# Router matrix stationary, rows' products first in the first expert, third expert from one-hot rows

## The chip, the cores and the metric

One core of a Trainium2 chip (trn2). The metric is the device time of one execution in microseconds. TensorE multiplies, VectorE (DVE), ScalarE (ACT) and GpSimd (POOL) compute elementwise, SyncE (SP) issues most of the transfers; POOL also issues all indirect ones (gather, scatter, scatter with add).

## The reference

One layer over 1024 tokens of width 1024, all float32: a mixer (short convolution, stick-breaking attention, gated linear attention), an output projection, a layer norm, then a mixture of experts and a second layer norm. What matters here:

```python
x = layer_norm(ALPHA * x + mix, ln1_g, ln1_b)         # mix = concatenated mixers @ w_out
scores = sigmoid(x @ router_w)                        # (1024, 16)
sel = scores + router_bias                            # best group of 4 by its two best; top 2 in it
gate = top-2 scores / their sum                       # zero for the other 14 experts
for e in range(16):
    h = silu(x @ w1[e]) * (x @ w3[e])                 # (1024, 512)
    y = y + gate[:, e:e+1] * (h @ w2[e])
out = layer_norm(ALPHA * x + y, ln2_g, ln2_b)
```

Only the two chosen experts of a token have a gate that isn't zero, so the kernel computes each expert for its own tokens alone. An output in float32 needs products more exact than one pass gives: a big product is made of three (hi x hi, hi x lo, lo x hi, with hi a rounded copy and lo the rest, lines 675 to 677, `mm3`).

## The kernel before

**Projection, first norm, router** (lines 887 to 924 on PE). Over the eight tiles of 128 tokens, iteration i of PE does: the eight transposes of tile i-2 of x1 (the normed x); 48 matmuls of the output projection of tile i; the router's product of tile i-2: x1T (128x128 per k) is stationary and 16 columns of the router's matrix `rw` move, eight calls. In float32 a call becomes two machine matmuls. ACT copies x1T out of PSUM between them, in a loop of its own order (lines 1255 to 1272); behind the last projection it also converts the first four weight pieces of expert 0 (`piece_hi`, 1.0 us each) ahead of the last x1T copy. `lg_ps` counts the tiles whose logits are there; at eight ACT takes the exponential (line 1276) and DVE begins the routing.

**Routing** (DVE, lines 1558 to 1635): sigmoid, ranks, masks, gates. Then PE counts each token's place in its expert (line 930), giving every token of an expert a slot: 160 slots for an expert, 128 "rows" (A) and 32 "spare" ones (B). For the first two experts a one-hot compare (`oneh`) and small PE products (lines 940 to 945) give the token of each slot at once (`firstA`, `firstB`), so that POOL gathers their x1 rows without the table. For all others the table `slot_tokens` in DRAM is written by 16 small indirect DMAs (`scatter`, line 569: a token's number and gate to its slot), and is read back by `load_table` (5 small DMAs for an expert), turned to indices by `quarters`, used by `gather`; `gates` puts the gates into `slotG`, and `add_rows` adds the expert's result to `sum_scratch` by two indirect DMAs (yB, yA).

**The experts** (`pe_block`, lines 981 to 1022). Each has 12 weight pieces of 512 KB: w1 (0 to 3), w3 (4 to 7), w2 (8 to 11). SP loads piece p of the next expert into the same raw buffer `er` as soon as the piece was split (`el_ok`) and read raw (`raw_done`). ACT makes `eh`, DVE `el`. PE does, in order: the spare rows' products with the raw weights (`spare_gu`, 64 calls = 128 small matmuls in four column groups, 32 of them each; raises `raw_done`), the rows' products with w1 and w3 (`rows_gu`, 24 big matmuls each), transposes of hB, of the next expert's gathered rows (rounds 0 and 1 of `x_transposes`), of hA, and of the next spare rows (round 2), then the products with w2, spare rows first (32 small ones) and then 24 big ones. Expert 0 is written out ahead of a loop over 1 to 14; expert 15 behind it. In the first block round 2 of the transposes comes first (`ROUNDS_FIRST = (2, 0, 1)`), since the spare rows' products only need that one. ACT's and DVE's order (`act_block`, `dve_block`) follow: pieces 4 and 5, then the spare rows' silu (which waits for `raw_done` of eight pieces) and multiply, then pieces 6 and on.

**POOL's order** behind the routing: gather of expert 0, scatter of the first choices (8 DMAs), gather of expert 1, scatter of the second choices, wait until the table has landed; then tables of experts 0, 1, 2, indices, gather 2, gates 0, adds of expert 0, and from there `step`: load table b, gates b-2, indices b, gather b, adds b-2. yA, yB and `slotG` are single buffers: ACT and DVE write the next expert's result once `y_out` says that the last one's adds have landed.

## Time and profile before

| what | value |
|---|---|
| runs shown | 1025.86 us median of 3 (1021.03 to 1026.15) |
| profiled execution | 1031.45 us, span 1029.6 us, mean granted clock 0.951 |
| PE busy | 933.0 us (91%) |
| DVE, ACT, POOL busy | 604.4, 475.6, 195.4 us |
| HBM | 142.84 MB read, 24.54 MB written |
| DMA queue of weights (q1) | 145.05 MB, 41.8% of 16 engines |

A row of a timeline is: start, duration, engine, line, operation, output<-inputs, shapes, how many, and in brackets how long the engine was idle ahead of it and what ended that. "issue" is idle time for which the trace shows no reason. PEld is the load of a stationary matrix, which runs beside PE. q1 is the queue of SP's transfers, q0 that of POOL's.

### The profile page before, as it was taken

Reading aid. Unit: us, or ns where it says so; the run is one execution under the profiler, and the core shown is the slowest. Engines: PE = TensorE matmul, PEld = TensorE weight load, DVE = VectorE, ACT = ScalarE, POOL = GpSimd, SP = SyncE. Lnnn points to the kernel's source line nnn. Section 1 sums busy time; section 2 is a strip of 40 time slices with the busy share of each in tenths; the row PEclk is TensorE's granted clock in tenths of the full one; section 3 lists DMA queues with packets and bytes.
Section 4 is the critical chain, followed back from the end, with each engine's and each line's share of the span. In section 5 each row is a group of like instructions: output and inputs, shape, how many; then the busy total and the mean of one; then the engine's idle time right before and its main releaser. Section 6 shows DMA issues by size and latency. Waiting matters only on the chain.

```text
span 1029.6 us, 18674 instructions
## 1 busy us (share of the span) xinstructions
PE 933.0 (91%) x7178; PEld 758.9 (74%) x7178; DVE 604.4 (59%) x786; ACT 475.6 (46%) x750; POOL 195.4 (19%) x238
## 2 busy tenths in 40 slices
PE   6998999998999999979998369999999999999940
PEld 5777988995777777768887338887888888888830
DVE  2301733654564655676556817777767777777728
ACT  3311432224554654561112126666666666666614
POOL 2000000000000000010000276333434334433116
PEclk9999999998999999989998569999999999999985
DMA  9301021001010031059332168999999999999656
GB/s 255 56 21 42 21 62 41 1 1 41 22 41 21 22 72 41 1 171 398 135 123 82 27 163 257 320 316 318 311 325 323 326 309 320 314 312 321 202 139 256
DMA packets 102659, 168.10 MB, mean 163 GB/s; under 512 B 25776, under 2 KB 49328, under 8 KB 102608
## 3 DMA queue, kind: packets, MB, share of 16 engines
q1 hardware_dynamic: 88768, 145.05, 41.8%
q0 software_dynamic: 10800, 21.17, 8.6%
q10 hardware_dynamic: 3040, 1.19, 0.5%
q8 instruction: 33, 0.54, 0.2%
q14 instruction: 18, 0.15, 0.0%
HBM read 142.84 MB, written 24.54 MB: 163 GB/s over the span
## 4 chain that ended last, share of the span: by engine, by line
PE 85%; DVE 7%; ACT 4%; DMA 2%; issue 2%; SPq 0%; POOL 0%; POOLq 0%; ACTq 0%; DVEq 0%
PE bank L675 13%; PE bank L677 12%; PE bank L676 12%; PE pz L675 8%; PE pz L677 7%; PE pz L676 7%; PE pz L966 6%; PE pz L1006 3%; PE pz L833 3%; PE bank L846 2%; PE bank L860 2%; PE bank L955 1%; PE bank L923 1%; DMA x_row<-in_x_dram 1%; DVE cstat L1679 1%
## 5 line engine op out<-in xcount | busy, mean ns | idle before, releaser
L1544 DVE TENSOR_TENSOR el<-er,eh 128x1024 fp32r<-128x1024 f32 x192 | 225.2, 1222 | 48.7 <-ACT eh L1253 48.4
L1253 ACT ACTIVATE eh<-er 128x1024 fp32r<-128x1024 f32 x192 | 190.3, 1051 | 0.0
L1477 DVE TENSOR_TENSOR_SCAN Qs<-Qs 128x128 f32<-128x128 f32 (+7 forms) x48 | 65.0, 1354 | 78.6 <-ACT Qs L1168 78.6
L675 PE MATMUL bank<-xT_hi,w_hi 128*128 128x512 f32 x256 | 105.4, 412 | 3.3 <-DVE xT_lo L1361 3.3
L675 PE MATMUL pz<-eh,xh 128*128 128x512 f32 x256 | 103.2, 403 | 2.3 <-issue 2.2
L677 PE MATMUL pz<-eh,xl 128*128 128x512 f32 x256 | 101.0, 395 | 0.4 <-issue 0.4
L676 PE MATMUL pz<-el,xh 128*128 128x512 f32 x256 | 101.2, 395 | 0.0
L677 PE MATMUL bank<-xT_hi,w_lo 128*128 128x512 f32 x256 | 101.1, 395 | 0.0
L676 PE MATMUL bank<-xT_lo,w_hi 128*128 128x512 f32 x256 | 101.0, 394 | 0.0
L544 POOL IOTA zidl<- 112x160 uint32 x1 | 0.3, 288 | 437.7 <-ACT aT L1179 437.7
L675 PE MATMUL bank<-w_hi,xT_hi 128*128 128x384 f32 x192 | 65.9, 343 | 6.8 <-DVE w_lo L1349 5.5
L966 PE MATMUL pz<-er,xB 128*32 128x128 f32 x2048 | 66.6, 279 | 5.3 <-issue 4.9
L966 PEld LDWEIGHTS pz<-er,xB 128*32 128x32 f32 x2048 | 57.2, 112 | 15.9 <-issue 15.4
L677 PE MATMUL bank<-w_hi,xT_lo 128*128 128x384 f32 x192 | 64.8, 338 | 0.0
L676 PE MATMUL bank<-w_lo,xT_hi 128*128 128x384 f32 x192 | 64.8, 338 | 0.0
L675 PEld LDWEIGHTS pz<-eh,xh 128*128 128x128 f32 x256 | 48.8, 191 | 17.0 <-issue 7.3
L675 PEld LDWEIGHTS bank<-xT_hi,w_hi 128*128 128x128 f32 x256 | 49.0, 191 | 13.9 <-DVE xT_lo L1361 3.9
L677 PEld LDWEIGHTS bank<-xT_hi,w_lo 128*128 128x128 f32 x256 | 48.7, 190 | 11.0
L677 PEld LDWEIGHTS pz<-eh,xl 128*128 128x128 f32 x256 | 48.9, 191 | 10.8 <-issue 0.4
L676 PEld LDWEIGHTS pz<-el,xh 128*128 128x128 f32 x256 | 48.9, 191 | 10.2 <-issue 0.9
L676 PEld LDWEIGHTS bank<-xT_lo,w_hi 128*128 128x128 f32 x256 | 49.0, 191 | 9.1
L675 PE MATMUL bank<-eh,hTh 128*128 128x512 f32 x128 | 51.7, 404 | 0.0
(264 smaller groups left out, 1794.9 us busy)
## 6 DMA issues: line engine op xcount, KB each, us to landing
er<-in_w_dram SPq DMA_DIRECT2D x192, 512.0 KB
w_raw<-in_w_in_dram SPq DMA_DIRECT2D x21, 512.0 KB, 3.8
x_row<-in_x_dram SPq DMA_DIRECT2D x8, 512.0 KB, 9.7
xres<-in_x_dram SPq DMA_DIRECT2D x8, 512.0 KB, 5.4
x_scratch<-x SPq DMA_DIRECT2D x8, 512.0 KB, 2.6
sum_scratch<-x SPq DMA_DIRECT2D x8, 512.0 KB, 4.0
cx<-sum_scratch SPq DMA_DIRECT2D x8, 512.0 KB, 6.4
out_dram<-cx SPq DMA_DIRECT2D x8, 512.0 KB, 2.6
```

The lines of the kernel that those rows point to most:

```text
L675: pe.matmul(dst, lh, rh, start=(k == k_first), stop=False)
L676: pe.matmul(dst, lh, rl, start=False, stop=False)
L677: last = pe.matmul(dst, ll, rh, start=False, stop=(k == k_last))
L833: pe.matmul(pz[h][:, c:e], q[r, 0, own], q[r, 1, c:e], start=True, stop=(e < W), skip_group_check=True)
L846: last = pe.matmul(po[64 * h:64 * h + 64, 0:P], sv[:, j, (2 * p + h) * SB_D:(2 * p + h + 1) * SB_D], aT[:, h, j, :], start=(j == 0), stop= ...
L860: last = pe.transpose(tr_bank[g % 2][:, (j % 4) * P:(j % 4 + 1) * P], Bs[:, n % 2, h, j * P:(j + 1) * P], ident[:, :])
L923: last = pe.matmul(pa_[:, c * NE:(c + 1) * NE], x1T[:, k, :], rw[:, k, :], start=(k == 0), stop=(k == NK - 1))
L966: last = pe.matmul(guB[g * TR:(g + 1) * TR, m * P:(m + 1) * P], xB[:, k, :], er[:, p, h * 512 + g * P:h * 512 + (g + 1) * P], start=(k == ...
L1006: last = pe.matmul(yB_bank[g * TR:(g + 1) * TR, :], hTB[:, f, :], er[:, p, g * DQ:(g + 1) * DQ], start=(f == 0), stop=(f == NF - 1), skip_ ...
L1253: act.activation(eh[:, p, :], er[:, p, :], ACT.Copy).then_inc(S["eh_ok"], 1)
L1477: dve.tensor_tensor_scan(Qs[:, h, 0:W][:, ::-1], Qs[:, h, 0:W][:, ::-1], Qs[:, h, 0:W][:, ::-1], 1.0, ALU.mult, ALU.min).then_inc(S["scan_ ...
L1544: dve.tensor_tensor(el[:, p, :], er[:, p, :], eh[:, p, :].bitcast(F32), ALU.subtract).then_inc(S["el_ok"], 1)
```

## The change

Four parts (`DIRECT` is 3).

The router: `rw` gets 32 columns (16 and 16 of zeros), is stationary, and x1T moves; call k goes to column group k % 4, so that four groups of 32 partitions of `po` hold partial logits, transposed. ACT copies them to `lgS`, and one more product with `gsum` (a 0/1 matrix made by POOL) adds the four groups and turns them back. That product for tile c comes one iteration later on PE, for the last tile at once.

The first block: rows first, spare rows last; round order (0, 1, 2).

The third expert gets its rows by one-hot as well; its compare, PE products (between the two `rows_gu`) and index arithmetic lie inside the first block. POOL gathers for it once expert 1's transposes are done, and reads the tables after that, in pairs.

The second expert's block is written out too, and has its own yA and yB.

```diff
+def sum_groups(c):
+    pe.wait_ge(S["lg_ev"], c + 1)
+    pe.matmul(pa_[:, c * NE:(c + 1) * NE], lgS[:, :], gsum[:, :], start=True, stop=True).then_inc(S["lg_ps"], 1)
...
+                if i >= 3:
+                    sum_groups(i - 3)
                 if i >= 2:
...
                     for k in range(NK):
-                        last = pe.matmul(pa_[:, c * NE:(c + 1) * NE], x1T[:, k, :], rw[:, k, :], start=(k == 0), stop=(k == NK - 1))
-                    last.then_inc(S["lg_ps"], 1)
+                        g = k % 4
+                        last = pe.matmul(po[TR * g:TR * g + TR, 0:P], rw[:, k, :], x1T[:, k, :], start=(k < 4), stop=(k >= NK - 4),
+                                         skip_group_check=True)
+                    last.then_inc(S["lgm_ps"], 1)
+            sum_groups(NT - 1)
...
-            def pe_block(b, nxt):
-                pe.wait_ge(S["xTh_ok"], NXR * b + (1 if first_block(b) else NXR))
-                spare_gu(b)
+            def pe_block(b, nxt, buf=0):
+                if not first_block(b):
+                    pe.wait_ge(S["xTh_ok"], NXR * b + NXR)
+                    spare_gu(b)
                 pe.wait_ge(S["xTl_ok"], 2 * b + 2)
                 rows_gu(b, 0)
+                if first_block(b):
+                    slot_tokens(2)
+                    pe.wait_ge(S["xTh_ok"], NXR)
                 rows_gu(b, 1)
+                if first_block(b):
+                    spare_gu(b)
...
+            def groups_out(c):
+                act.wait_ge(S["lgm_ps"], c + 1)
+                if c >= 1:
+                    act.wait_ge(S["lg_ps"], c)
+                act.activation(lgS[:, :], po[:, 0:P], ACT.Copy).then_inc(S["lg_ev"], 1)
             for i in range(NT + 2):
                 if i + 1 < NT:
                     mix_hi(i + 1)
+                if i >= 3:
+                    groups_out(i - 3)
...
-            for b in range(2):
-                pool.wait_ge(S["first_ok"], 2 * b + 2)
+            for b in range(DIRECT):
+                if b < 2:
+                    pool.wait_ge(S["first_ok"], 2 * b + 2)
                 if b:
-                    scatter(0)
+                    scatter(b - 1)
+                if b == 2:
+                    pool.wait_ge(S["first_ok"], 2 * b + 2)
+                if b:
                     pool.wait_ge(S["xtr_ps"], NXR * b)
...
-            scatter(1)
...
-                for e in range(3):
-                    load_table(e, b0 + e)
...
+                load_table(0, b0)
+                load_table(1, b0 + 1)
+                quarters(0, b0, 2)
+                quarters(1, b0 + 1)
...
                 gates(0, b0)
-                add_rows(0, b0)
-                step(3, b0 + 3)
+                if isinstance(j, int):
+                    add_rows(0, b0)
+                    gates(1, b0 + 1)
+                load_table(2, b0 + 2)
+                load_table(3, b0 + 3)
+                quarters(2, b0 + 2, 2)
+                quarters(3, b0 + 3)
...
+                gather(3, b0 + 3)
+                add_rows(1, b0 + 1, 1)
...
             block(NE * j, True)
-            with eng.Fori(1, NE - 1) as e:
+            block(NE * j + 1, True, 1)
+            with eng.Fori(2, NE - 1) as e:
                 block(NE * j + e, True)
```

On ACT and DVE the first block's silu and multiply for the spare rows move behind pieces 10 and 11 and the rows' multiply; all else keeps its place.

## Rows read from the trace of the kernel before

**Rows 1.** The page's head.
```profile
span 1029.6 us, 18674 instructions
```

**Rows 2.** Windows by stage: bounds, length, busy us of each engine, clock, DMA share, GB/s.
```profile
475.00:554.00 79.00, 79.00 (x415) 67.62 (x413) 43.02 (x59) 12.79 (x23) 0.00 (x0) 1.00 0.45 170
...
587.20:603.10 15.90, 10.67 (x129) 5.49 (x128) 3.61 (x4) 3.77 (x4) 12.24 (x13) 0.71 0.74 187
603.10:621.70 18.60, 15.86 (x48) 11.17 (x49) 7.19 (x7) 6.45 (x8) 13.25 (x21) 0.69 0.37 103
...
631.00:654.90 23.90, 23.90 (x248) 19.39 (x247) 16.81 (x18) 15.55 (x21) 12.16 (x12) 1.00 0.97 323
```

**Rows 3.** The chain that ended last: start, us, what; two router products.
```profile
486.53 1.69 PE bank L923 x16
...
500.05 1.69 PE bank L923 x16
```

**Rows 4.** Timeline of PE at the start of the second block.
```profile
630.98 3.70 PE L966 MATMUL pz<-er,xB 128*32 128x128 f32 x128
634.61 0.50 PE L675 MATMUL pz<-eh,xh 128*128 128x512 f32 x1
634.95 0.40 PE L676 MATMUL pz<-el,xh 128*128 128x512 f32 x1
635.18 0.39 PE L677 MATMUL pz<-eh,xl 128*128 128x512 f32 x1
```

**Rows 5.** Timeline behind the last projection: ACT and PE.
```profile
557.92 3.89 ACT L1253 ACTIVATE eh<-er 128x1024 fp32r<-128x1024 f32 x4
...
562.54 1.02 ACT L1266 ACTIVATE x1T<-pz 128x1024 f32<-128x1024 f32 x1 [0.73 <-PE pz L894]
...
563.61 3.60 PE L923 MATMUL bank<-rw,x1T 128*128 128x16 f32 x16 [1.11 <-ACT x1T L1266]
567.25 0.28 ACT L1276 ACTIVATE rs<-bank 128x128 f32<-128x128 f32 x1 [3.69 <-PE bank L923]
```

**Rows 6.** Timeline of PE in the first block.
```profile
587.18 5.44 PE L966 MATMUL pz<-er,xB 128*32 128x128 f32 x88
592.92 0.44 PE L966 MATMUL pz<-er,xB 128*32 128x128 f32 x5 [0.30 <-issue]
...
602.43 0.65 PE L966 MATMUL pz<-er,xB 128*32 128x128 f32 x4 [0.34 <-issue]
603.86 0.59 PE L675 MATMUL pz<-eh,xh 128*128 128x512 f32 x1 [0.79 <-issue]
...
612.38 0.58 PE L675 MATMUL pz<-eh,xh 128*128 128x512 f32 x1 [0.48 <-issue]
```

**Rows 7.** Timeline of the other engines in the first block.
```profile
586.17 1.04 POOL L569 DMA_INDIRECT slot_tokens<-tokg,rows_u  x1 [4.02 <-DVE rows_u L1629]
...
587.92 0.69 DVE L1550 TENSOR_TENSOR xl<-bank,xh 128x512 fp32r<-128x512 f32 x1 [0.16 <-ACT xh L1283]
...
589.67 45.29 SPq L380 DMA_DIRECT2D er<-in_w_dram  x17
...
609.20 0.98 POOL L569 DMA_INDIRECT slot_tokens<-tokg,rows_u  x1 [0.30 <-issue]
```

**Rows 8.** All DMA queues between 608 and 614 us: packets, MB, share of 16 engines.
```profile
q0 software_dynamic: 128, 0.00, 1.8%
```

**Rows 9.** Timeline of POOL and ACT around the first blocks' ends.
```profile
624.34 1.07 POOL L607 DMA_INDIRECT xgA<-x_scratch,tab  x1 [1.07 <-PE pz L955]
...
626.72 0.31 POOL L612 COPY slotG<-tab 128x2 f32<-128x2 f32 x1
...
636.40 1.26 POOL L592 DMA_DIRECT2D tab<-slot_tokens  x1
...
646.36 0.26 POOL L600 TENSOR_SCALAR tabQ<-tab,quad 128x1 uint32<-128x1 uint32 x1 [5.69 <-DMA tab<-slot_tokens]
...
651.29 0.48 ACT L1309 ACTIVATE yB<-pz,slotG 128x256 f32<-128x256 f32 x1 [1.72 <-remote]
```

More of the change, by code:

```diff
@@ L124 @@
 AHEAD = NF
+DIRECT = 3
 BIG = float(1 << 20)
@@ L231, in small @@
             return t
-        rw = small("rw", [P, NK, NE])
+        rw = small("rw", [P, NK, TR])
+        lgS = small("lgS", [P, P])
+        gsum = small("gsum", [P, NE])
         rb = small("rb", [P, NE])
@@ L543, in _ @@
             pool.wait_ge(S["conv_ok"], 10)
+            pool.memset(rw[:, :, NE:], 0.0).then_inc(S["gsum_ok"], 1)
+            pool.memset(gsum[:, :], 0.0).then_inc(S["gsum_ok"], 1)
+            for g in range(4):
+                pool.wait_ge(S["gsum_ok"], 2 + g)
+                pool.affine_select(gsum[:, :], gsum[:, :], [[-1, NE]], ALU.not_equal, 1.0, base=-TR * g, channel_multiplier=1)\
+                    .then_inc(S["gsum_ok"], 1)
             pool.iota(zidl[:, :, 0], [[1, TW]], base=T, channel_multiplier=0).then_inc(S["tokc_ok"], 1)
@@ L641, in pool_pass @@
                 b0 = NE * j
-                for e in range(3):
-                    load_table(e, b0 + e)
-                for e in range(3):
-                    quarters(e, b0 + e, 3 - e)
-                    if e == 2 or not isinstance(j, int):
-                        gather(e, b0 + e)
-                gates(0, b0)
-                add_rows(0, b0)
-                step(3, b0 + 3)
+                load_table(0, b0)
+                load_table(1, b0 + 1)
+                quarters(0, b0, 2)
+                quarters(1, b0 + 1)
+                if not isinstance(j, int):
+                    gather(0, b0)
+                    gather(1, b0 + 1)
+                gates(0, b0)
+                if isinstance(j, int):
[5 more added lines that the diff above has]
+                quarters(3, b0 + 3)
+                if not isinstance(j, int):
+                    gather(2, b0 + 2)
+                    add_rows(0, b0)
+                    gates(1, b0 + 1)
+                gather(3, b0 + 3)
+                add_rows(1, b0 + 1, 1)
                 with pool.Fori(1, NE // 4) as i:
@@ L1295, in act_block @@
                 piece_hi(b, 11)
+                if first_block(b):
+                    spare_silu()
                 act.wait_ge(S["hTB_ps"], b + 1)
@@ L1596, in _, with slot_rows @@
                                   skey[:, b, :].unsqueeze(2).to_broadcast([P, NT, TW]), ALU.is_equal).then_inc(S["oneh_ok"], 1)
-            for b in range(2):
+            def slot_rows(b):
+                bank = sids_bank[b % 2]
                 dve.wait_ge(S["sids_ps"], b + 1)
                 for c in range(2):
-                    dve.tensor_copy(sids[:, 2 * b + c:2 * b + c + 1], sids_bank[b][c][:, 0:1]).then_inc(S["sids_ok"], 1)
+                    dve.tensor_copy(sids[:, 3 * b + c:3 * b + c + 1], bank[c][:, 0:1]).then_inc(S["sids_ok"], 1)
@@ L1606, in _ @@
                                          ALU.mult, ALU.add).then_inc(S["sids_ok"], 1)
                 dve.wait_ge(S["sids_ok"], 3 * b + 3)
-                dve.tensor_scalar(firstB[:, b:b + 1], sids[:, 4 + b:5 + b], float(NQ), quad[:, 0:1], ALU.mult, ALU.add).then_inc(S["first_ok"], 1)
+                dve.tensor_scalar(firstB[:, b:b + 1], sids[:, 3 * b + 2:3 * b + 3], float(NQ), quad[:, 0:1], ALU.mult, ALU.add)\
+                    .then_inc(S["first_ok"], 1)
+            for b in range(2):
+                slot_hits(b)
@@ L1610, in _ @@
+            for b in range(2):
+                slot_rows(b)
             link(dve.tensor_reduce(rmax[:, :], rpos[:, NT, :], AX.X, ALU.max))
```

86 lines of the change are left out of this document (54 added, 32 removed).

## The prediction

> **What bounds the kernel now.** I read the page's head first: a span of 1029.6 us in an execution of 1031.45 us [rows 1]. The runs shown have a median of 1025.86 us, 5.6 us less; sums are made against the profiled execution and the difference is then taken off that median. The windows by stage come next [rows 2]. In the stage of the output projection (475 to 554 us) TensorE is busy 79.00 of 79.00 us, so a column less there is time. In a steady expert (631 to 654.9) it is busy 23.90 of 23.90 us at clock 1.00, with a DMA share of 0.97: TensorE sets the pace and the transfers keep up. The first expert is different. The products that take 3.7 us [rows 4] and about 11 us in a steady expert take from 587.2 to 621.7 us, 34.5 us in place of 14.7, with the clock at 0.71 and 0.69 [rows 2]. That is the largest hole, and the timeline of it is the third view: the first 88 products of the spare rows run closed up, the other 40 come in bundles until 603 us, and then twelve of the 128 rows' products take from 603.86 to 612.38 us [rows 6]. Over the same stretch GpSimd issues sixteen small indirect writes of the slot table and one gather pair, from 586.17 to 610.2 us, one each 1.3 us, and the loads of the second expert's weights run from 589.67 us [rows 7]. Between 608 and 614 us the DMA queues hold only the small writes (1.8% of the engines), and TensorE still limps [rows 8]; at 612.38 it is free.
>
> **The router's products.** Before, x1T is stationary: 16 matmuls and 16 loads of 128x128 for a tile of tokens, 1.69 us each time [rows 3]. Now eight calls with a 32-column stationary go to four column groups, 128 columns moving: again 16 machine matmuls, with the shape of the spare rows' products, 128 of which take 3.70 us [rows 4], so 16 take 0.46 us. The sum over the groups adds one call, two matmuls of the old kind: 2/16 of 1.69 = 0.21 us. [Rows 4] also show what a change of tile shape costs: the first big product after the spare rows' starts 0.34 us before the next one, the following ones are 0.23 apart, so 0.11 us; there are two changes for a tile. Per tile 1.69 - 0.46 - 0.21 - 0.22 = 0.80 us. The period of the stage is 13.52 us [rows 3], all of it TensorE's, and five of the eight tiles' router products stand ahead of the last projection: 5 x 0.80 = 4.0 us. The bounds are 0 (the groups don't overlap: four at a time now take 4 x 0.029 = 0.116 us, and 16 of those are 1.85 us, the old price) and 5.2 us (no cost of a change). ScalarE's new copy for a tile (0.28 us, as other 128x128 copies) lies in a stage where ScalarE is mostly idle.
>
> The Trainium skill bears on both sides of this. "TensorEngine Tiling (Array Packing)", Performance Considerations, advises the swap of stationary and streaming side where the streamed side has few columns, with four column tiles; its Key Properties say that a change of tiling mode drains TensorE. The 0.11 us of [rows 4] agrees with the second, as a price that eats a fifth of the gain.
>
> **The tail of the router.** Behind the last projection the chain is: ScalarE's copy of the last transposes at 562.54, router products 563.61 to 567.21 at half clock, exponential at 567.25 [rows 5]. ScalarE is in order, and two group copies now stand ahead of that: one ahead of the sixth tile's x1T copy (0.3 us), one that waits for the seventh tile's router products ahead of the four weight conversions of 3.89 us [rows 5]. I cost them at 0.3 and 0.5 us: the last copy begins at 563.3. Then 1.0 copy, 1.0 products (0.46 at half clock, and their tail), 0.35 group copy, 0.7 sum at half clock with its change: exponential at about 566.5, 0.7 earlier. The one-hot keys of the second expert now stand between the two compares, and the first slot rows come 0.2 us later. Net -0.5 (from -1.5 to +1). Router in all: -4.5 us.
>
> **The first expert.** Times below are in the frame of the old trace. Spare products could begin at 587.18; rows' products need both halves of xl, the second of which ends at 588.61 [rows 7]: TensorE begins 1.3 us later. Then come 24 products, the 80 small instructions of the third expert's slot tokens, 24 products, the 128 of the spare rows, and a new exposed round (last spare product, silu, multiply, transpose: 0.85 us), since the spare rows' hidden values used to be ready long before. What does the stall do to this? From 592.92 to 603 TensorE gets through 40 products, 4 a microsecond with their loads, [rows 6]; a full-clock 128-row product needs 0.23 us [rows 4], 4.3 a microsecond. So a long product hides what a short one can't: first 24 in about 6.6 us, to 595.1. And no piece of the raw weights is given back before the spare rows have read it, so the loads that began at 589.67 [rows 7] wait until then, and the stall has only the small writes in it. I take it that TensorE then runs nearly free: slot tokens 1 us, second 24 in 5.6 to 601.7; then the spare rows, with the loads starting under them while small writes go on until 610.2 [rows 7], are held until the stall's end at 612.4 and close at 613.5; with 0.85 that is 614.3 against 621.7: -7.4 us. The bounds: no stall at all, 601.7 + 3.7 + 0.85 = 606.2, -15.5 us; the stall as now and slot tokens caught in it at 3 to 4 a microsecond (40 in 10 to 13 us, to 607), six rows' products by 612.4, 18 behind (5 us with some at half clock), 3.7 and 0.85: 622, +0.3, at worst +2.
>
> Weights for the second expert: the 4.2 MB of its first eight pieces, at the 323 GB/s of a steady expert [rows 2], are there 13 us after the first spare product; the second block begins 14 us after it and reads the last of them 17 us after. The other four pieces run some 2 us further into the second block than now, which needs them later still. Nothing waits.
>
> The Trainium skill, "Runtime: NRT & Kernel Launch", Instruction fetch mechanics, says that TensorE's instructions are streamed in 16 KiB blocks ahead of use and that the cost of a block is mostly hidden. By that rule an unrolled second block costs nothing and the stall isn't code loading; [rows 8] agree as far as they go, with TensorE stalled and no instruction queue at work.
>
> **GpSimd's chain.** It now waits for the second expert's transposes before the third gather and only then reads the first two tables. With t as the start of the spare rows: transposes done t+6.3, gather until t+8.7 (2.4 us for the pair from 624.34 on, to the gates at 626.72 [rows 9]), ten table loads and their landing 14 us (five took 10.0, 636.40 to 646.36 [rows 9]), slot rows and gates 1, first expert's two adds 9.7 at most (626.72 to 636.40 [rows 9]), so the second expert's gates at t+33.4. ScalarE wants them for yB 20.3 us into the second block (651.29 against 631 [rows 9]), t+34.5. That is 1 us of slack. The fourth gather comes 16.4 us after (two tables again, 2.4), t+50, and its rows are wanted by the third block's end phase at t+53; a landing takes some 4 to 8 us (the tables' takes 10 less the issue [rows 9]). I put 1 us on it, bounds 0 and 5.4. The own buffers for the second expert's result take away its wait for the first's adds, which does not show in the old trace: nothing.
>
> **Sum.** -4.5 - 7.4 + 1.0 = -10.9: profiled execution 1020.5, median 1025.86 - 10.9 = 1015 us.
>
> **Rivals.** (a) *The small writes alone make the stall.* For it: [rows 8], a stall with no weights moving. Against: 88 products ran freely beside the first four writes [rows 6, 7]. Then the first expert gives between 0.3 late and 3 early, by how much of the stall the slot tokens fill, say 1.4: -4.5 - 1.4 + 1 = -4.9, 1021, with a spread of -3 to -6.5. (b) *The stall goes wholly*, the loads being its cause: it starts within a microsecond of 589.67. -4.5 - 15.5 + 1 = -19: 1007. (c) *The stall belongs to the profiled execution only.* The timed runs are 5.6 us shorter. Then the new order only costs 1.3 + 0.85 + 0.7 there, router -4.5, 1 for GpSimd: -0.7, 1025. (d) *Slower: GpSimd's chain sets the pace.* Its place is the wait for the transposes ahead of the tables. It decides from the point where the way to the second gates takes over 28.2 us, against 27 in my sum. If a round of two tables takes 20 us (twice the five of [rows 9]) in place of 14, the second expert's gates are 5 late, the fourth gather 6 + 5 late beyond the 5.4 above; TensorE waits some 14 us in the third block, -4.5 - 3 + 14: 1032.
>
> **How the numbers follow.** Chances: forecast 0.36, (a) 0.28, (b) 0.16, (c) 0.09, (d) 0.11. A measurement of this kernel tells 0.5% (5.1 us) from no change. The forecast and (b) are faster; of (a), with its spread about the bound, 0.17 falls on the faster side: 0.69. Same: the rest of (a) and (c), 0.20. Slower: (d), 0.11. The range takes in (b) without its lowest end and (c) without (d): 1004 to 1026.
>
> **What would show it.** The router's group between the projections: 0.5 us for 16 matmuls and a period near 12.7 us; if the period is 13.5, the groups don't overlap. In the first expert: products every 0.23 us from about 592, clock 1.00, second block near 619 in the old frame; if rows' products come three in 2.1 us as now, (a) is right. Before the third block: TensorE waiting for a gather, or ScalarE's yB for gates, is (d). Weights late anywhere in the second block would make me wrong where I costed nothing.

## The result and the profile after

| kernel | median, us | runs | ratio to before | 95% interval |
|---|---|---|---|---|
| before | 1027.12 (1021.03 to 1030.49) | 20 | | |
| after | 1020.93 (1017.87 to 1025.71) | 20 | 0.9943 | 0.9927 to 0.9960 |

The change makes the kernel 0.57% faster, 5.9 us by the ratio. Against the 1025.86 us of the forecast's frame that is 1020.0; the forecast was 1015.0, 10.9 us faster: right in sign, and nearly twice too large. The sign is the router's (e1 below); the part of the forecast that lay in the first expert's block, -7.4 us, didn't come. The profiled execution took 1025.71 us, and the page's head answers to [rows 1], with a span 5.5 us shorter:

```profile
span 1024.1 us, 18771 instructions
```

**The router** answers to [rows 3] in two pieces of the chain of waits (start, us, what):

```profile
501.46 0.57 PE bank L960 x16
502.03 1.02 PE pz L926 x8
...
514.10 0.57 PE bank L960 x16
514.67 1.02 PE pz L926 x8
```

The sixteen products take 0.57 us for 1.69, and the period is 514.10 - 501.46 = 12.64 us for 13.52. The tail behind the last projection answers to [rows 5] (timeline: start, duration, engine, line, and in brackets the idle time ahead and what ended it):

```profile
560.70 1.01 ACT L1325 ACTIVATE x1T<-pz 128x1024 f32<-128x1024 f32 x1
561.76 1.08 PE L960 MATMUL bank<-x1T,rw 128*32 128x128 f32 x16 [1.29 <-ACT x1T L1325]
562.91 0.28 ACT L1310 ACTIVATE lgS<-bank 128x128 f32<-128x128 f32 x1 [1.20 <-PE bank L960]
563.24 0.61 PE L917 MATMUL bank<-gsum,lgS 128*128 128x16 f32 x2 [0.40 <-ACT lgS L1310]
563.89 0.28 ACT L1336 ACTIVATE rs<-bank 128x128 f32<-128x128 f32 x1 [0.70 <-PE bank L917]
```

The exponential comes at 563.89 for 567.25. In this execution the attention stage ended 2.3 us later than in the one of before (the transposes of x1's first tile start at 476.89 for 474.60), which is no part of the change, so the router gave 5.6 us.

**The first block** answers to [rows 6] (timeline of PE):

```profile
585.23 0.80 PE L703 MATMUL pz<-eh,xh 128*128 128x512 f32 x1 [1.18 <-DVE xl L1617]
585.82 0.63 PE L704 MATMUL pz<-el,xh 128*128 128x512 f32 x1
...
590.51 0.42 PE L703 MATMUL pz<-eh,xh 128*128 128x512 f32 x1
...
593.90 0.50 PE L703 MATMUL pz<-eh,xh 128*128 128x512 f32 x1
...
599.57 3.70 PE L1010 MATMUL pz<-er,xB 128*32 128x128 f32 x128
603.99 0.33 PE L1039 MATMUL pz<-ident,hB 128*128 128x128 f32 x1 [0.72 <-DVE hB L1720]
```

Twelve products at half clock (0.43 us apart, granted clock 0.50 from 585.2 to 590.5), the others 0.23 apart, the spare rows' 128 in one piece: 18.8 us to the transposes of hB for 34.5. Here the stall is gone wholly. Then it is given back. The second block answers to [rows 4]:

```profile
613.31 2.39 PE L1010 MATMUL pz<-er,xB 128*32 128x128 f32 x80
616.62 0.64 PE L1010 MATMUL pz<-er,xB 128*32 128x128 f32 x16 [0.92 <-DMA er<-in_w_dram]
621.23 1.08 PE L1010 MATMUL pz<-er,xB 128*32 128x128 f32 x16 [3.97 <-DMA er<-in_w_dram]
622.48 1.08 PE L1010 MATMUL pz<-er,xB 128*32 128x128 f32 x16 [0.17 <-DMA er<-in_w_dram]
...
662.54 1.97 PE L999 MATMUL bank<-ident,xgA 128*128 128x128 f32 x8 [3.27 <-DMA xgB<-x_scratch,tabQ]
```

The second expert's weights are late (5.1 us of waits and a stretch at half clock), and at the third block's end the fourth expert's rows are late. The windows between the transposes of hB, one for each block, answer to [rows 2] (bounds, length, busy us of PE, PEld, DVE, ACT, POOL, clock, DMA share, GB/s):

```profile
585.20:604.00 18.80, 18.05 (x217) 14.70 (x217) 12.23 (x17) 9.06 (x11) 15.14 (x13) 0.86 0.24 58
604.00:635.10 31.10, 26.05 (x248) 20.22 (x249) 16.85 (x17) 15.57 (x21) 18.20 (x23) 0.95 1.02 317
635.10:659.00 23.90, 23.90 (x248) 19.39 (x247) 17.45 (x18) 15.65 (x21) 16.02 (x18) 1.00 0.98 327
659.00:687.90 28.90, 25.63 (x248) 20.71 (x247) 17.54 (x18) 15.64 (x21) 16.01 (x20) 0.94 0.92 271
```

Against 23.9 for a steady block, two blocks are 7.2 and 5.0 us too long. From POOL's first gather to the fourth hB this execution needs 111.2 us, before needed 113.6. The table below has that sum for every run. It comes from one execution each and leaves the router out, so it shows where time went and doesn't rank kernels.

### The profile page after: what moved, and what is told of

The parts are those of the page before. It is cut to its first block, busy times and chain, and to the rows that moved or that the text cites. A ratio compares the mean times of both kernels' runs of the same rounds, so it can differ in the third digit from the quotient of the medians.

```text
span 1024.1 us, 18771 instructions
## 1 busy us (share of the span) xinstructions
PE 922.9 (90%) x7234; PEld 751.7 (73%) x7234; DVE 607.5 (59%) x793; ACT 476.3 (47%) x758; POOL 201.9 (20%) x244
## 4 chain that ended last, share of the span: by engine, by line
PE 78%; DVE 7%; DMA 4%; ACT 4%; POOL 4%; issue 3%; SPq 0%; POOLq 0%; ACTq 0%; DVEq 0%
PE bank L703 13%; PE bank L705 12%; PE bank L704 12%; PE pz L703 6%; PE pz L705 6%; PE pz L704 6%; PE pz L1010 5%; PE pz L861 3%; PE pz L1056 3%; PE bank L874 2%; PE bank L888 2%; PE bank L999 1%; POOL slot_tokens L579 1%; DMA tab<-slot_tokens 1%; DVE cstat L1766 1%
## 5 line engine op out<-in xcount | busy, mean ns | idle before, releaser
L1010 PE MATMUL pz<-er,xB 128*32 128x128 f32 x2048 | 60.7, 276 | 5.1 <-DMA er<-in_w_dram 5.1
L703 PEld LDWEIGHTS pz<-eh,xh 128*128 128x128 f32 x256 | 48.9, 191 | 14.6 <-issue 3.2
L705 PEld LDWEIGHTS pz<-eh,xl 128*128 128x128 f32 x256 | 48.8, 191 | 10.4
```

The source lines that it names most:

```text
L703: pe.matmul(dst, lh, rh, start=(k == k_first), stop=False)
L705: last = pe.matmul(dst, ll, rh, start=False, stop=(k == k_last))
L1010: last = pe.matmul(guB[g * TR:(g + 1) * TR, m * P:(m + 1) * P], xB[:, k, :], er[:, p, h * 512 + g * P:h * 512 + (g + 1) * P], start=(k == ...
```

## The experiments

Every kernel ran beside the kernel before on the same chip, and ratios are to that one. The e runs are from one chip, the h runs from a second, the f, g and i runs from a third. The table has the blocks of each profile: the time from POOL's first gather to the first transpose of hB, and from there to the second, third and fourth.

| kernel | ratio (95%) | to hB 1 | 2 | 3 | 4 | sum |
|---|---|---|---|---|---|---|
| before | 1 | 41.9 | 23.9 | 23.9 | 23.9 | 113.6 |
| after | 0.9943 (0.9927 to 0.9960) | 27.3 | 31.1 | 23.9 | 28.9 | 111.2 |
| g0_after_again | 0.9971 (0.9943 to 0.9998) | 39.5 | 25.8 | 23.9 | 29.1 | 118.4 |
| e1_router | 0.9936 (0.9914 to 0.9959) | 33.9 | 26.4 | 24.6 | 28.2 | 113.1 |
| e2_rows_first | 1.0013 (0.9986 to 1.0040) | 38.2 | 24.0 | 27.3 | 28.3 | 117.8 |
| e3_loads_held | 1.0016 (0.9981 to 1.0051) | 45.2 | 32.0 | 24.3 | 24.0 | 125.5 |
| e4_writes_held | 1.0090 (1.0059 to 1.0120) | 23.8 | 38.9 | 34.9 | 27.1 | 124.8 |
| f1_no_router | 1.0008 (0.9985 to 1.0030) | 39.4 | 24.5 | 23.9 | 24.1 | 111.9 |
| f2_tables_first | 0.9945 (0.9922 to 0.9967) | 39.5 | 25.9 | 24.7 | 24.5 | 114.6 |
| f3_spare_middle | 0.9991 (0.9963 to 1.0019) | 43.5 | 23.9 | 23.9 | 24.1 | 115.5 |
| f4_writes_beside_rows | 1.0037 (1.0017 to 1.0058) | 24.2 | 24.3 | 40.2 | 34.8 | 123.6 |
| g1_writes_one_run | 0.9930 (0.9904 to 0.9957) | 24.2 | 31.6 | 23.9 | 33.9 | 113.6 |
| g2_both_gates_late | 0.9922 (0.9894 to 0.9950) | 24.4 | 31.6 | 24.5 | 28.0 | 108.5 |
| g3_second_eight_held | 0.9918 (0.9891 to 0.9944) | 27.5 | 29.7 | 30.0 | 24.6 | 111.7 |
| h1_after_no_writes | 0.9876 (0.9851 to 0.9902) | 27.3 | 25.3 | 23.9 | 23.9 | 100.5 |
| h2_before_no_writes | 0.9861 (0.9836 to 0.9886) | 23.6 | 23.9 | 24.0 | 23.9 | 95.4 |
| h3_rows_64_bytes | 1.0069 (1.0043 to 1.0096) | 27.3 | 24.0 | 23.9 | 31.2 | 106.4 |
| h4_order_undone | 0.9941 (0.9916 to 0.9965) | 24.9 | 31.4 | 23.9 | 27.4 | 107.6 |
| i1_before_64_bytes | 1.0012 (0.9988 to 1.0035) | 38.2 | 27.9 | 23.9 | 23.9 | 114.0 |
| i2_combined | 0.9882 (0.9854 to 0.9911) | 25.0 | 31.7 | 23.9 | 23.9 | 104.5 |

### The parts of the change

**e1_router**: of the change the router part alone (with `sum_groups`, `groups_out` and `gsum`).

```diff
+pe.matmul(po[TR * g:TR * g + TR, 0:P], rw[:, k, :], x1T[:, k, :], ...)
```

> Only the router's part of the change (stationary matrix of 32 columns, four column groups, one product more for the sum); first block, tables and buffers as before. If the parts are independent: the period of a token tile in the projection stage falls from 13.52 to about 12.64 us, the exponential comes some 5 us earlier, the first block is stalled as before (second block starts some 44 us behind the first spare product), the time falls by 4.5 to 5.5 us, a ratio of 0.9950. Rival: the parts interact, an earlier routing meets the stall at another place and the time moves by less than 2 or more than 8 us.

0.9936, for an expected 0.9950 that lies inside the interval: the router alone gives the whole of the measured gain.

**e2_rows_first**: of the change the first block's order alone (PE's, ACT's and DVE's).

```diff
-ROUNDS_FIRST = (2, 0, 1)
+ROUNDS_FIRST = (0, 1, 2)
...
                 rows_gu(b, 1)
+                if first_block(b):
+                    spare_gu(b)
```

> Only the order of the first block (rows' products first, spare rows' last, with ScalarE's, VectorE's and the round order to match); router, tables, third expert and buffers as before. Theory: the order alone takes the stall away, the first block is 14 us shorter, the second expert waits for its weights some 7 us because their loads can't start before the spare rows' products; the third expert's gather is early, as the tables are read before it, so nothing is lost there, but the second expert's result must wait for the single buffers. Ratio 0.993 (-7 us, from -4 to -9). Rival: the third expert's direct gather is what gains, then this kernel is not faster than before.

1.0013, not 0.993: nothing that these runs can tell from zero, and the order alone doesn't take the stall away. The rows' products run free, but here the spare rows' meet the second eight writes and take from 599.64 to 614.7 us.

**f1_no_router**: the change without its router part.

```diff
-pe.matmul(po[TR * g:TR * g + TR, 0:P], rw[:, k, :], x1T[:, k, :], ...)
+pe.matmul(pa_[:, c * NE:(c + 1) * NE], x1T[:, k, :], rw[:, k, :], ...)
```

> The change without its router part: products' order in the first block, one-hot rows for the third expert, own buffers for the second. Theory N (the net gain of the change is the router's; the order frees up to 17 us in the first block and 12 us of it come back in the next two): ratio to before 0.998 to 1.003, first hB transpose some 15 us earlier than before's 621.7 or, where the spare products meet the second batch of writes, 6 us earlier, and the third about level. Rival O (order and direct rows are worth 3 us or more by themselves, router and they overlap): ratio below 0.997.

1.0008, as theory N has it; with e1, 0.9936 x 1.0008 = 0.9944, the change's 0.9943. Order, third expert's one-hot rows and the buffers are together worth nothing beyond the interval, which is -1.5 to +3.1 us.

**h4_order_undone**: the change with the first block's order of before.

```diff
-ROUNDS_FIRST = (0, 1, 2)
+ROUNDS_FIRST = (2, 0, 1)
...
-                if first_block(b):
-                    spare_gu(b)
```

> The changed kernel with the first block's order of before (router, third expert's one-hot rows and second buffers kept). Theory N (the net is the router's, 0.9936 by itself, and the other parts give nothing together): 0.992 to 0.996. If the rows-first order is a loss once the weights are late, 0.988 to 0.991; if it carries some of the gain, above 0.997.

0.9941: the order is worth nothing inside the change either. The profile shows more. With the old order, and the first writes issued at 581.25, this execution has no stall (timeline of PE):

```profile
582.32 5.74 PE L1010 MATMUL pz<-er,xB 128*32 128x128 f32 x128
...
605.51 1.97 PE L999 MATMUL bank<-ident,xgA 128*128 128x128 f32 x8 [5.49 <-DMA xgB<-x_scratch,firstB]
```

So an execution can escape the stall in either order. And what the free first block gains (24.9 us to hB for 41.9) goes in part at once: TensorE waits 5.5 us for the second expert's rows, whose gather stands behind the first eight writes and goes out at 594.17.

**g0_after_again**: the changed kernel unaltered.

> The changed kernel unaltered, profiled a second time. Theory V (whether the first block's spare products are stalled beside the second eight small writes varies from execution to execution, and the time hardly follows it, because in this order the weights of the second expert start to load with these products and land no earlier than some 22 us later): ratio 0.993 to 0.997; where the profile shows a stall, the first hB transpose comes at 610 to 616 for 604, but the second at 635 to 640 and the fourth at 686 to 690 as before. Rival: the fourth comes as much later as the first.

0.9971, a little above the expected range, and its interval overlaps the first one's. The transposes of hB come at 611.0, 636.8 and 689.9, as theory V has them. The profile now has the stall that the first one lacked (timeline of PE; three of the pieces, and the end):

```profile
593.89 1.78 PE L1010 MATMUL pz<-er,xB 128*32 128x128 f32 x50
595.95 0.39 PE L1010 MATMUL pz<-er,xB 128*32 128x128 f32 x3 [0.28 <-issue]
...
600.30 0.38 PE L1010 MATMUL pz<-er,xB 128*32 128x128 f32 x2 [1.01 <-issue]
...
606.74 3.58 PE L1010 MATMUL pz<-er,xB 128*32 128x128 f32 x51 [1.49 <-issue]
```

Same program, 12.2 us more in the first block, 5.3 less in the second: part of the stall lies over the wait for weights that there would have been without it. One profile was not enough to say that the stall "goes".

### What the stall is

**e3_loads_held**: before, SP starts the second expert's loads only when the first block is done.

```diff
+            sp.wait_ge(S["hTB_ps"], 1)
             with sp.Fori(1, NE) as e:
                 load_expert(sp, 0, e)
```

> The kernel before, with one wait more: SyncE starts no load of the second expert's weights until the first block's hB transpose, that is behind all its gate and up products. Theory L (the stall needs the weight loads beside the small table writes): spare products close in about 6 us from 587.2, rows' products run at 0.23 us, the transposes come near 605 in place of 621.7; the weights then come late in the second block, so the time is -4 to -8 us. Theory W (the small table writes alone make it): the first block is stalled as before and the late weights come on top: +3 to +8 us.

The profiled execution took 1048.91 us, 8.7 more than the median of this kernel's runs, so only its order of events is used. The ratio, 1.0016 (0.9981 to 1.0051), can't tell the theories apart. The stall stays with no weights moving: the DMA queues from 595 to 612 us, and a piece of PE's timeline in it:

```profile
q0 software_dynamic: 553, 0.67, 19.8%
q14 instruction: 1, 0.01, 0.1%
```
```profile
590.53 3.50 PE L967 MATMUL pz<-er,xB 128*32 128x128 f32 x56
...
611.33 0.37 PE L967 MATMUL pz<-er,xB 128*32 128x128 f32 x1 [0.84 <-issue]
```

**e4_writes_held**: before, the sixteen writes held until the first block is done.

```diff
-                    scatter(0)                # ahead of gather 1
...
+            pool.wait_ge(S["hTB_ps"], 1)
+            scatter(0)
             scatter(1)
```

> The kernel before, with GpSimd's sixteen small table writes held until the first block's hB transpose (gathers of both first experts go out ahead). Theory W (the small writes are needed for the stall): first block unstalled, transposes near 604; the tables come some 10 us late relative to the blocks, and the third expert waits for its gather: first block 17 us shorter, 10 to 15 us given back. Theory L without writes (the loads alone stall it): first block as before, near 621, and the tables come 20 us late on top: +15 us or more.

The first block is free (16.4 us) and the stall goes where the writes go, into the second:

```profile
611.33 0.77 PE L967 MATMUL pz<-er,xB 128*32 128x128 f32 x12
613.23 0.45 PE L967 MATMUL pz<-er,xB 128*32 128x128 f32 x4 [1.12 <-issue]
...
626.36 3.36 PE L967 MATMUL pz<-er,xB 128*32 128x128 f32 x57 [0.79 <-issue]
```

The tables are then late as well: 1.0090, or 9.3 us slower, where theory W had the first block's gain mostly given back and no more.

The stall isn't TensorE's alone. In before ScalarE's silu of the spare rows needs only products that ended at 603.08, and starts at 612.58, when the stall ends; VectorE, which waits for it, stands still too (timeline of ACT):

```profile
612.58 0.28 ACT L1289 ACTIVATE silB<-pz 128x128 f32<-128x128 f32 x1 [21.50 <-remote]
```

**h2_before_no_writes** and **h1_after_no_writes**: both kernels without the sixteen writes and the wait for them (the table keeps its filled-in ids, so the experts read from it get no tokens).

```diff
-                for i in range(NT):
-                    pool.indirect_dma_start(idl_dram, bass.IndirectOffsetOnAxis(rows_u[:, c, i:i + 1], 0), tokg[:, c, i, :], ...)
+                pass
```

> The kernel before without its sixteen small writes (left out as in the other). Theory W: its spare products come first and free the weights' buffers at 588, so blocks follow each other in 24 us: hB transposes near 604, 628, 652, 676 in spite of the slower router, ratio 0.981 to 0.985, not behind the changed kernel without writes. Rival (the stall of 17 us is not the writes' doing, but of the first run through that code or of the start of the loads): first hB transpose at 615 to 622 as before and ratio above 0.99.

> The changed kernel without its sixteen small writes of slot_tokens (left out: the tables hold only the filled-in spare ids, so no expert after the third gets its tokens). Theory W (in the new order the weights of the second expert start to load with the spare products, near 598, and take some 22 us, whatever the writes do): hB transposes near 603, 631 to 633, 655 and 680, of which the second block still holds 5 us or more of waits for er; ratio to before 0.986 to 0.991. Rival S (the writes are all that the new order suffers from): 603, 627, 651, 675 and ratio 0.981 to 0.985.

Before without writes: 0.9861, 14.3 us of its 1026.4. That is what the writes cost, stall and the wait for the tables together. After without writes: 0.9876, that is 6.9 us less than after's 0.9943, and 9.8 less than g0's 0.9971 for the same kernel. So the writes seem to cost the changed kernel less, about half to two thirds; whether the order does that isn't shown, for no run has the old order inside the change without writes. And yet the two kernels without writes are level, although one has the faster router. The two profiles say where that goes; before without writes, then after without writes (PE):

```profile
588.86 0.66 PE L953 MATMUL pz<-ident,xgB 128*128 128x128 f32 x2 [5.80 <-DMA xgB<-x_scratch,firstB]
...
591.16 5.34 PE L964 MATMUL pz<-er,xB 128*32 128x128 f32 x128
596.43 0.50 PE L673 MATMUL pz<-eh,xh 128*128 128x512 f32 x1
...
607.46 0.27 PE L987 MATMUL pz<-ident,hB 128*128 128x128 f32 x1
```
```profile
579.53 0.79 PE L701 MATMUL pz<-eh,xh 128*128 128x512 f32 x1 [1.03 <-DVE xl L1615]
...
593.87 3.70 PE L1008 MATMUL pz<-er,xB 128*32 128x128 f32 x128
598.29 0.33 PE L1037 MATMUL pz<-ident,hB 128*128 128x128 f32 x1 [0.72 <-DVE hB L1718]
...
612.03 0.64 PE L1008 MATMUL pz<-er,xB 128*32 128x128 f32 x16 [0.80 <-DMA er<-in_w_dram]
```

From the first gather to hB the new order takes 27.3 us for 23.6 (it begins 1.1 us later behind its transposes, has twelve long products at half clock where the old one has the spare rows' at 5.34 for 3.70, the slot tokens inside, and 0.7 for the exposed silu and multiply), and the second block is 1.4 us longer by late weights. With nothing stalled the changed blocks cost 5.1 us more in these two executions, about what the router gives.

h1's ratio lies in theory W's range, but theory W itself (late weights come from the order) falls by the last row: without writes the wait is 0.8 us, not 5 or more. In after the DMA engines moved 271 GB/s from the loads' start at 600.5 to 622.5, in h1 334 from 594.8 to 612.0. But in h3 (next), with eight writes beside the loads' start as in after, it was 357 GB/s from 608.5 to 625 and no weight was late. So it isn't shown that writes beside the loads are enough to delay them.

**h3_rows_64_bytes** and **i1_before_64_bytes**: each table row in 64 bytes of its own, in after (filled late) and in before (filled during attention).

```diff
-        idl_dram = nc.dram_tensor("slot_tokens", [NROW, 2], U32).ap()
+        idl_rows = nc.dram_tensor("slot_tokens", [NROW * 8, 2], U32).ap()
+        idl_dram = idl_rows.rearrange("(r w) o -> r (w o)", w=8)[:, 0:2]
...
-                dve.tensor_copy(rows_u[:, c, :], rr12[:, c, :])
+                dve.tensor_scalar(rows_u[:, c, :], rr12[:, c, :], 8.0, None, ALU.mult)
```

> The changed kernel with each 8-byte row of slot_tokens in 64 bytes of its own (indices times 8; the fill before in seven transfers). Theory M (writes of neighbouring rows fall into the same piece of memory, and everything that reads memory waits for them): no stall in the spare products of either block and the small writes land at once, ratio 0.987 to 0.991. Rival D (GpSimd's making of the descriptors, not where they write, holds the others): issue gaps of TensorE as in the other profiles, ratio 0.993 to 0.998.

> The kernel before with each 8-byte row of slot_tokens in 64 bytes of its own, filled in seven transfers during the attention stage; nothing else changed. Theory M (only where the small writes go matters, not that GpSimd makes their descriptors): the first block is 16.5 to 18 us for 34.5 though the writes are still issued beside its spare products, the second 24; part of it comes back because the tables are still read after the writes; ratio 0.986 to 0.992, not far from 0.9861 without any writes. Rival D (the clean profile of the changed kernel with such rows was chance): stall of over 8 us in the first block, ratio 0.996 or more.

h3's profile has no stall and no late weights, but it was slower (1.0069): its first gather came at 584.69 for 576.68. The fill of 17,920 small pieces, issued from 450.78 to 517 us, lies in the router's stage, and I take it for the reason; that wasn't tested. i1, with the fill put away, has the stall as ever and 1.0012:

```profile
586.94 5.47 PE L971 MATMUL pz<-er,xB 128*32 128x128 f32 x100
592.68 0.40 PE L971 MATMUL pz<-er,xB 128*32 128x128 f32 x2 [0.27 <-issue]
...
599.37 0.39 PE L971 MATMUL pz<-er,xB 128*32 128x128 f32 x1 [0.83 <-issue]
```

So giving each row 64 bytes of its own doesn't take the stall away (theory M falls), and h3's clean profile was an execution without the stall, as after's first was.

### Attempts at keeping the gain

**f2_tables_first**: after, all four tables read ahead of the first adding of rows.

```diff
+                    load_table(2, b0 + 2)
+                    load_table(3, b0 + 3)
+                    for e in range(4):
+                        quarters(e, b0 + e, 4 - e)
```

> After with GpSimd's tables of the third and fourth expert read together with the first two's, ahead of the first adding of rows, so that the fourth expert's gather needs no table read behind that adding. Theory G (the late gather costs the 5 us by which the third block was too long in after's profile, 28.9 for 23.9): that block falls to 24 to 25 us, span and time 4 to 5 us less than after's, ratio to before about 0.990. Rival S (the weights' stream is the second limit and takes most of it back): ratio 0.993 to 0.995, the wait goes to weights' loads in that block or the next.

The third-to-fourth step falls to 24.5 us from 28.9, as theory G says. The ratio, 0.9945, not the expected 0.990, lies between those of after's two measurements: any gain is inside the intervals. It is rival S's number without its reason, for no wait for weights is in this profile, only 5.5 us of issue idle in the stall.

**f3_spare_middle**: after, spare rows' products between the two halves.

```diff
                     slot_tokens(2)
                     pe.wait_ge(S["xTh_ok"], NXR)
+                    spare_gu(b)
                 rows_gu(b, 1)
```

> After with the first block's spare products between the two halves of the rows' products: the weights' buffers come free 5.5 us earlier (loads of the second expert from about 595 for 600.5). Theory W (the second block's 7 us are weights that land late because the order lets them start 10.8 us later): the wait of the second block's spare products falls to 2 us or less and the block by 5 to 6; if the spare products are then not slowed by the first batch of writes, ratio to before about 0.989. Rival: the spare products, now beside the writes, are stretched by 5 to 13 us as in before, and ratio is 0.992 to 0.996.

The rival: spare rows' products at 593.89 to 614.7 beside the writes, 43.5 us to the first hB, no wait for weights in the second block (23.9). At 0.9991 it came out worse than the rival's 0.992 to 0.996.

**f4_writes_beside_rows**: after with the order of before; first eight writes when the first block's spare rows' products are done, the other eight when the second's are.

```diff
+                if b:
+                    pool.wait_ge(S["raw_done"], 2 * NF if b == 1 else NPIECE + 2 * NF)
+                    scatter(b - 1)
```

> After with the first block's order of before (spare products first), and the small writes moved instead: the first eight start when the spare products of the first block are done, the other eight when those of the second are, and each gather goes ahead of the writes that stood before it. Theory B (long 128x512 products bear the writes, short spare products don't, and only the spare products free the weights' buffers): loads of the second expert start near 585, first block 16 to 18 us with its hB transpose near 599, second near 624, ratio to before 0.980 to 0.988. Rival T (the tables are late: GpSimd reads them 10 us later, the gates and gathers behind them hold the second and third block): ratio 0.990 to 1.000, waits of ScalarE for the gates and of TensorE for the fourth expert's gather.

Two clean blocks (24.2, 24.3), and then the row of the waits (engine, line, waited for: us, times, longest):

```profile
ACT yB L1367 <- POOL slotG L623: 22.1, 1, 22.1
```

The gates come at 647 us, and 1.0037 is above even rival T's range. Late tables cost more than the stall did.

**g1_writes_one_run**: the same without the second hold; **g2_both_gates_late**: besides (the last lines of the diff), POOL gates the second block's rows too, four tables read together, fourth gather first.

```diff
+                if b == 1:
+                    pool.wait_ge(S["raw_done"], 2 * NF)
+                    scatter(0)
+                    scatter(1)
...
+        def gated_late(b):
+            return isinstance(b, int) and b < 2
```

> The kernel with spare products first and writes beside the rows' products, but the second eight writes follow the first without a hold (the hold kept the gates of the second block back by 22 us in the run before). Theory B and T together (block order and weights are good, only the tables were late): writes end at 610 for 624, the gates of the second block come at about 638 for 647, ScalarE's wait for them 12 to 14 us for 22, fourth hB transpose 685 to 689 for 697, ratio 0.992 to 0.997. Rival: the spare products of the second block, at 607 to 611, meet the end of the writes and are stalled by over 5 us, and nothing is gained: ratio 1.000 or more.

> The same, and GpSimd gates the second block's rows too, as it does the first's (their own buffers allow it), with all four first tables read together and the fourth expert's gather ahead of the adding. Theory B (the first three blocks then wait for no table, and the weights start at 583): hB transposes near 598, 623, 648 and 672 to 676, ratio 0.982 to 0.987. Rival W (the weights' stream, at 0.9 or more of the DMA engines from 585 on, allows no block under 24 us and the tables' small reads land late behind it): fourth transpose 680 to 686, ratio 0.988 to 0.993.

0.9930 and 0.9922: g1's is in its range, g2's is in rival W's, where theory B had 0.982 to 0.987. The first block is free up to hB, though seven of g2's writes fall in it; the others meet the products with w2. In g2 (timeline of PE, then of ACT):

```profile
603.52 0.50 PE L713 MATMUL bank<-eh,hTh 128*128 128x512 f32 x1
604.45 0.39 PE L714 MATMUL bank<-el,hTh 128*128 128x512 f32 x1 [0.42 <-issue]
...
613.04 0.49 PE L713 MATMUL bank<-eh,hTh 128*128 128x512 f32 x1 [0.32 <-issue]
```
```profile
615.94 0.38 ACT L1379 ACTIVATE yB<-pz 128x256 f32<-128x256 f32 x1 [11.58 <-remote]
```

The long products limp as the short ones do (24 of them from 603.52 to 613.93, 10.4 us, for the 5.7 from 607.64 to 613.31 in after), and ScalarE, which needed only products that ended at 603.6, starts at 615.94.

**g3_second_eight_held**: f2 with the second eight writes held until the first block's spare rows' products are done.

```diff
                 if b == 2:
+                    pool.wait_ge(S["raw_done"], 2 * NF)
```

> The changed kernel with tables first, and its second eight small writes held until the first block's spare products are done, so that these are never beside writes. Theory W (in the rows-first order the weights decide, not the stall): first hB transpose at 601 to 604 without a stall, second still at 632 to 636, and the ratio is no better than 0.992. Rival S (the stall decides): second at 626 to 628 and ratio 0.982 to 0.986.

0.9918: the time that W predicted, but not for its reason. Its second block has only one wait for weights (0.50 us) and a stalled stretch at 614.9 to 618.5; in the third ScalarE's yB waits 10.7 us for the gates.

**i2_combined**: router, third expert direct, order of before, second gather ahead of the writes, 64-byte rows filled early, four tables read together, own gate buffer for the second block.

```diff
+        slotGs = [small("slotG", [P, 2]), small("slotG1", [P, 2])]
...
+                    gates(0, b0)
+                    gates(1, b0 + 1, 1)
+                    gather(3, b0 + 3)
                     add_rows(0, b0)
```

> The changed kernel with the first block's order of before, the second expert's gather ahead of the small writes, 64-byte rows filled early, four tables read together and a gate buffer of its own for the second block. If the router's 6 us, the missing stall and the tables add up: first block near 17 us, no late weights or gathers, ratio 0.976 to 0.982. If the tables or the adding of rows hold the second or third block by 5 us or more: 0.983 to 0.988.

0.9882 (0.9854 to 0.9911): better than both kernels, 12.2 us below before, but short of 0.976 to 0.982, and what holds it isn't the tables or the adds of the other range. The first block is free (17.6 us from its first product to hB); the second again has a stall (31.7 us, its spare rows' products from 611.32 to 622.8), and the step from the fourth hB to the fifth is 4.8 us too long.

## Why the prediction was too high, step by step

Two steps failed: the -7.4 us of the first expert, which the new order was to bring, and "nothing waits" behind it. What came is the router's gain alone.

**The router's products**: right, if somewhat low. Forecast -0.80 a tile, measured -0.88 in the period; the stage and its tail -5.6 us against -4.5 in the profile, -6.6 in the timed runs (e1, -4.2 to -8.9). The 16 products take 0.57 us for an estimate of 0.46, the sum and the changes of shape less than I put on them (and the upper bound of 5.2 us is 5.1 by its own terms). The rule of the Trainium skill on the swap ("TensorEngine Tiling (Array Packing)", Performance Considerations) holds here, as a gain of 0.64% of the kernel.

**The first expert, "a long product hides what a short one can't"**: wrong, and the main step that failed. My own [rows 6] spoke against it already: twelve long products took from 603.86 to 612.38 us, 0.71 each, where 0.23 is their price at full clock. I compared a rate of short products in the stall with a rate of long ones outside it. g2 has long products limping too; in f4 they run free beside writes, and in after and h4 both kinds do. So what is stalled is not set by the kind of product. The term was also worked out from one execution of before, with a stall of fixed length. g0 ran as I had described it, rows' products free and spare rows' held until the writes were out, and its first hB came 2.4 us sooner than before's, not 7.4; after's first profile had no stall, and there it came 14.6 sooner. By the fourth hB g0 is 4.8 us behind before's one and after's first profile 2.4 ahead. In the timed runs the order is worth nothing that they can tell from zero: e2 1.0013, f1 1.0008, and h4, which undoes it, 0.9941 for 0.9943.

**The new order's own price**: rival (c) had it at 1.3 + 0.85 + 0.7 = 2.85 us. Without any writes it is 3.7 us in the first block and 1.4 in the second, 5.1, by one profile of each kernel. Together with the late gather that is enough to use up what the writes' price falls by, 7.4 us (14.3 to 6.9; by g0's ratio 4.5).

**"Nothing waits" for the weights**: wrong for after's profile by 7.2 us. I took 323 GB/s and 13 us for eight pieces; they took 22 us in after (600.5 to 622.4, writes beside them until 610.2), and some 17 without writes (594.8 to 612.0, h1). A rate read in a steady block did not hold in the block where the loads begin. In g0, where the first block ends 7 us later, no weight is late.

**GpSimd's chain, 1.0 us of 0 to 5.4**: the fourth gather was late by 5.0 and 5.2 us in after's two profiles, near the upper bound. The second expert's gates came 38.9 us after the spare rows' start for the forecast's 33.4, but ScalarE waited only 0.3 us for them, since its block was late too. f4 shows its other end: one more hold of 8.5 us and ScalarE waits 22.1.

**Rivals**: (a), that the small writes alone make the stall, is what e3, e4 and h2 show, and its 1021 us was the time. That number is partly luck: it had -4.5 for the router and -0.4 for all else, where e1 gives -6.6 and f1 +0.8. (b) falls with e3: the stall stays without loads. (c) falls by h2: the writes' price is in the timed runs too, 14.3 us where the profiles have 18.2 (113.6 for 95.4), though it varies. (d) was right in its place, too high in its price.

**Shown**: the net is the router's (e1, f1, h4); the stall comes from GpSimd's sixteen indirect writes (e4, h2), and needs neither the loads (e3) nor rows that share 64 bytes (i1). **Open**: by what way the writes hold TensorE and ScalarE at once, and why some executions escape: of the profiles with writes three, after, h3 and h4, have no stall. In ten of the profiles the stall begins behind 7 to 100 small products that ran closed up, and then lets bundles of mostly 1 to 6 through, mostly 0.7 or 1.4 us apart. That would fit a supply of instructions that runs dry, but no run tested it: the trace shows 0.1% of instruction transfers in e3's stretch. In f4, g1 and g2 the 56th small product starts 0.21 to 0.26 us late before any write is issued, while the second expert's gather goes out, so a gap of that size needs no write.

## What to carry to other kernels

Where two stalls or waits compete for one stretch, measure first what is left when their cause is absent altogether (here one run without the writes): it bounds every rearrangement, and it showed that the new order had a price of its own. A block that ends 18 us sooner brings its next weights, tables and gathers into question: price each against the earlier start, with the slowest landing seen and not the steady one. And profile a kernel twice before a gap of one execution becomes a term of a sum.

## What was unexpected of the hardware

Sixteen indirect writes of 1 KB each (one instruction of 0.98 us each 1.29 us on GpSimd) cost this kernel 14.3 us of 1026.4 (h2; the stall and the wait for the table together), while between 608 and 614 us they kept the DMA engines 1.8% busy [rows 8]. GpSimd's own instruction takes 1.97 us at times (after, four in a row from 585.67 us, with VectorE at work from 586.69 to 593.58) and 0.98 at others (before, from 592.38, with VectorE standing still). In g2 a ScalarE instruction began 12 us after its operands were ready while the writes went on. Four column groups of a 32-column stationary run 16 products in 0.57 us where the other orientation takes 1.69.
